# A softmax in a transformer layer divides its probabilities before they are turned, and its transposed inverse goes away

## The reference, cut to what matters

```python
def forgetting_attention(q, k, v, log_f):
    cum = jnp.cumsum(log_f, axis=-1)
    ...
        logits = jnp.einsum('bhqd,bhkd->bhqk', q_i, k).astype(jnp.float32) * scale
        logits = logits + c_i[..., :, None] - cum[..., None, :]
        logits = jnp.where(pos_i[:, None] >= kpos[None, :], logits, -jnp.inf)
        p = jax.nn.softmax(logits, axis=-1)
        return jnp.einsum('bhqk,bhkd->bhqd', p.astype(v.dtype), v)
```

## Time and profile before

| | |
|---|---|
| Time, median of 3 executions | 1922.04 us (1921.72 to 1925.91) |
| Profiled execution | 1924.92 us, its span 1923.2 us |
| Busy over the span | PE 98%, DVE 62%, POOL 44%, ACT 39% |
| Span of the attention's four pairs | about 780 to 970 us |
| Granted clock of PE over the span | 0.996 of full speed |

### The profile page before, as it was taken

The page is one execution under the profiler, slowest core; times in us unless marked ns, Lnnn a source line. Parts: engine busy times, 40 slices in busy tenths (PEclk is TensorE's granted clock), DMA queues, the critical chain, the costliest instruction groups (busy, mean ns, idle before and its releaser), DMA issues. The chain is left out here.

```text
span 1923.2 us, 25334 instructions
## 1 busy us (share of the span) xinstructions
PE 1881.0 (98%) x9240; PEld 1545.9 (80%) x9240; DVE 1184.5 (62%) x1720; ACT 758.4 (39%) x1389; POOL 842.9 (44%) x629
## 2 busy tenths in 40 slices
PE   7999999999999999999999999999999999999998
PEld 6878888888888877777788887877888888888886
DVE  6876666665777792455515567577453445358778
ACT  5632232222444442555513554244333233334445
POOL 1587777774000011222211242489887788700003
PEclk9999999999999999999999999999999999999999
DMA  9246656654976310311112112622422333168662
GB/s 346 76 142 188 202 176 203 187 169 135 350 261 193 122 40 22 133 45 45 67 33 72 55 43 93 216 98 89 132 103 90 103 117 109 39 262 324 207 193 92
DMA packets 211946, 267.93 MB, mean 139 GB/s; under 512 B 14558, under 2 KB 125426, under 8 KB 211314
## 3 DMA queue, kind: packets, MB, share of 16 engines
q1 hardware_dynamic: 211826, 266.34, 41.4%
HBM read 211.16 MB, written 53.03 MB: 137 GB/s over the span
## 5 line engine op out<-in xcount | busy, mean ns | idle before, releaser
L470 POOL TENSOR_TENSOR ffn_ring_b<-ffn_raw_in,ffn_ring_b 128x512 fp32r<-128x512 f32 x146 | 207.3, 1427 | 113.0 <-ACT ffn_ring_b L465 113.0
L1127 PE MATMUL bank<-ffn_w_hi,ffn_a_hi 128*128 128x512 f32 x616 | 240.2, 390 | 1.3 <-DVE ffn_w_lo L1093 1.2
L1129 PE MATMUL bank<-ffn_w_hi,ffn_a_lo 128*128 128x512 f32 x616 | 239.7, 389 | 0.0
L1128 PE MATMUL bank<-ffn_w_lo,ffn_a_hi 128*128 128x512 f32 x616 | 239.7, 389 | 0.0
L111 POOL TENSOR_SCALAR rms<-rms 128x1 f32<-128x1 f32 x20 | 9.4, 470 | 435.6 <-ACT ffn_junk L103 421.6
L465 ACT CAST ffn_ring_b<-ffn_raw_in 128x512 fp32r<-128x512 f32 x150 | 92.5, 621 | 217.6 <-PE bank L1652 210.8
L1082 ACT CAST ffn_a_hi<-ffn_a_stage 128x512 fp32r<-128x512 f32 x154 | 95.6, 621 | 199.0 <-PE bank L1129 194.2
L470 POOL TENSOR_TENSOR ffn_ring_a_lo<-ffn_raw_in,ffn_ring_a_hi 128x512 fp32r<-128x512 f32 x106 | 146.1, 1390 | 55.5 <-ACT ffn_ring_a_hi L465 53.4
L1441 DVE TENSOR_TENSOR ffn_u<-bank,ffn_u 128x512 f32<-128x512 f32 x106 | 72.9, 688 | 126.4 <-PE bank L1652 126.1
L1093 DVE TENSOR_TENSOR ffn_a_lo<-ffn_a_stage,ffn_a_hi 128x512 fp32r<-128x512 f32 x154 | 106.2, 690 | 68.5 <-ACT ffn_a_hi L1082 68.3
L1127 PEld LDWEIGHTS bank<-ffn_w_hi,ffn_a_hi 128*128 128x128 f32 x616 | 115.6, 188 | 26.9 <-DVE ffn_w_lo L1093 2.0
(11 more groups left out here) (416 smaller groups left out, 4725.3 us busy)
## 6 DMA issues: line engine op xcount, KB each, us to landing
ffn_raw_in<-in_w_ffn_in SPq DMA_DIRECT2D x84, 512.0 KB, 5.8
ffn_a_stage<-hidden SPq DMA_DIRECT2D x154, 256.0 KB, 3.2
ffn_w_stage<-in_w_ffn_out SPq DMA_DIRECT2D x132, 256.0 KB, 3.1
ada_rest<-in_w_ada SPq DMA_DIRECT2D x64, 448.0 KB, 4.0
hidden<-ffn_u SPq DMA_DIRECT2D x87, 256.0 KB, 2.0
hidden<-ffn_g SPq DMA_DIRECT2D x66, 256.0 KB, 2.0
mx_raw_w<-in_w_mix_in SPq DMA_DIRECT2D x28, 512.0 KB, 4.4
xres<-in_x SPq DMA_DIRECT2D x16, 512.0 KB, 8.5
```

What stands on the lines that cost most here:

```text
L470: pool.tensor_tensor(self.lo(q), self.source(b, m), self.hi(q).bitcast(F32), ALU.subtract)\
L1127: pe.matmul(dst, a_hi, w_hi, start=first, stop=False, skip_group_check=True)
L1128: pe.matmul(dst, a_hi, w_lo, start=False, stop=False, skip_group_check=True)
L1129: return pe.matmul(dst, a_lo, w_hi, start=False, stop=True, skip_group_check=True)
```

## The change

Each tile of probabilities is divided by its row sums on DVE, in place, between the exponential and the turning: `scale_prob(p, n)` waits for `exp_rows`, takes the inverse of one column of `rowsum`, waits for it, and multiplies the tile. `turn_prob` waits for this (`prob_scaled`) and no longer for the exponential. `invert`, `turn_rinv` and `keep_rinv` are gone, with the semaphores of theirs, and `normalise` becomes `keep_y_fox`, a copy. On PE, steps 2 to 5 are written like steps 6 and 7: values first, then both turnings.

```diff
-            def keep_rinv(p, q, first):
-                act.wait_ge(pv_ready, p * NS + (q + 1))
...
-                act.copy(rinv[:, 2 + q % 2, :], core.bank[:, 6 + q % 2, P:2 * P]).then_inc(rinv_kept, 1)
...
-            def invert(p, q, first):
...
-                dve.reciprocal(rinv[:, q % 2, :].rearrange("p (e d) -> p e d", e=2),
-                               rowsum[:, 2 * q:2 * q + 2].unsqueeze(2).to_broadcast([P, 2, HD]))\
-                    .then_inc(rinv_made, 1)
+            def scale_prob(p, n):
+
+                dve.wait_ge(prob_done, p * PER + (n + 1))
+                rows = prob[:, n % RP, 0:(BLOCK[n] + 1) * P]
+                link(dve.reciprocal(rinv[:, n:n + 1], rowsum[:, n:n + 1]))
+                dve.tensor_scalar(rows, rows, rinv[:, n:n + 1], None, ALU.mult).then_inc(prob_scaled, 1)
...
+            def keep_y_fox(p, q):
                 i = BLOCK[2 * q]
...
+                dve.tensor_copy(yT_fox[:, bass.ds(p, 1), i * P:(i + 1) * P].rearrange("p a s -> p (a s)"),
+                                core.bank[:, 6 + q % 2, 0:P]).then_inc(y_done, 1)
 
             def fox_body(p, first, last):
                 link.at(p)
                 for q in range(1, NS + 1):
                     if not last and q < NS and q - 1 in STEP_OF:
                         cut_qk(p + 1, STEP_OF[q - 1])
+                    scale_prob(p, 2 * q - 2)
                     if q < NS:
                         logits(p, 2 * q, first)
+                    scale_prob(p, 2 * q - 1)
                     keep_pt(p, 2 * q - 2, first)
                     if q < NS:
                         logits(p, 2 * q + 1, first)
-                    invert(p, q - 1, first)
                     keep_pt(p, 2 * q - 1, first)
...
             def turn_prob(p, n, first):
                 i = BLOCK[n]
-                pe.wait_ge(prob_done, p * PER + (n + 1))
+                pe.wait_ge(prob_scaled, p * PER + (n + 1))
...
-            def turn_rinv(p, q):
-                bank = core.bank[:, 6 + q % 2, :]
-                pe.wait_ge(rinv_made, p * NS + (q + 1))
-                pe.transpose(bank[:, P:2 * P], rinv[:, q % 2, :], core.ident[:, :]).then_inc(pv_ready, 1)
...
                     scores(p, q, first)
-                    if q in (6, 7):
+                    if q == 1:
+                        turn_prob(p, 0, first)
+                        project_q0(p, first, range(KD - 2, KD))
+                    else:
                         values(p, q - 2, first)
-                        turn_rinv(p, q - 2)
                         turn_prob(p, 2 * q - 2, first)
-                    else:
-                        turn_prob(p, 2 * q - 2, first)
-                        if q == 1:
-                            project_q0(p, first, range(KD - 2, KD))
-                        else:
-                            values(p, q - 2, first)
-                            turn_rinv(p, q - 2)
                     turn_prob(p, 2 * q - 1, first)
```

More of the change, by code:

```diff
@@ L1872, in mixer @@
     pv_ready, y_done = s("pv_ready"), s("y_done")
-    rinv_made, rinv_kept = s("rinv_made"), s("rinv_kept")
+    prob_scaled = s("prob_scaled")
     x_ready, x_kept = s("x_ready"), s("x_kept")
@@ L1917, in mixer @@
     rowsum = fsb("rowsum", [P, 2 * NS])
-    rinv = core.at("mx_rinv", [P, 4, P], 120)
+    rinv = fsb("rinv", [P, 2 * NS])
     wait_tile = fsb("wait_tile", [P, 2 * NS])
@@ L2227, in keep_pt @@
                 act.copy(pt_of(n, 0, w), turned_bank(n, 0)[:, 0:w]).then_inc(pt_act, 1)
-            def keep_rinv(p, q, first):
-                act.wait_ge(pv_ready, p * NS + (q + 1))
-                if not (first and q < 2):
-                    act.wait_ge(y_done, p * NS + (q - 1))
-                act.copy(rinv[:, 2 + q % 2, :], core.bank[:, 6 + q % 2, P:2 * P]).then_inc(rinv_kept, 1)
             def fox_body(p, first, last):
@@ L2423, in keep_pt @@
                 dve.tensor_copy(pt_of(n, BANK, w), core.bank[:, 5, 0:w - BANK]).then_inc(pt_dve, 1)
-            def invert(p, q, first):
-                dve.wait_ge(prob_done, p * PER + (2 * q + 2))
-                if not (first and q < 2):
-                    dve.wait_ge(pv_ready, p * NS + (q - 1))
-                dve.reciprocal(rinv[:, q % 2, :].rearrange("p (e d) -> p e d", e=2),
-                               rowsum[:, 2 * q:2 * q + 2].unsqueeze(2).to_broadcast([P, 2, HD]))\
-                    .then_inc(rinv_made, 1)
-            def normalise(p, q):
-                dve.wait_ge(rinv_kept, p * NS + (q + 1))
+            def scale_prob(p, n):
[4 more added lines that the diff above has]
+            def keep_y_fox(p, q):
                 i = BLOCK[2 * q]
-                dve.tensor_tensor(yT_fox[:, bass.ds(p, 1), i * P:(i + 1) * P].rearrange("p a s -> p (a s)"),
-                                  core.bank[:, 6 + q % 2, 0:P], rinv[:, 2 + q % 2, :], ALU.mult).then_inc(y_done, 1)
+                dve.wait_ge(pv_ready, p * NS + (q + 1))
+                dve.tensor_copy(yT_fox[:, bass.ds(p, 1), i * P:(i + 1) * P].rearrange("p a s -> p (a s)"),
+                                core.bank[:, 6 + q % 2, 0:P]).then_inc(y_done, 1)
             def fox_body(p, first, last):
@@ L2456, in fox_body @@
                     if q > 1:
-                        normalise(p, q - 2)
-                normalise(p, NS - 1)
+                        keep_y_fox(p, q - 2)
+                keep_y_fox(p, NS - 1)
                 if not last:
@@ L2703, in values @@
                     for e in range(2):
-                        pe.matmul(bank[e * HD:(e + 1) * HD, 0:P], v_fox[:, j, bass.ds(p * (2 * HD) + e * HD, HD)],
-                                  pt_of(2 * q + e, j * P, (j + 1) * P), start=(j == 0), stop=(j == i))
-            def turn_rinv(p, q):
-                bank = core.bank[:, 6 + q % 2, :]
-                pe.wait_ge(rinv_made, p * NS + (q + 1))
-                pe.transpose(bank[:, P:2 * P], rinv[:, q % 2, :], core.ident[:, :]).then_inc(pv_ready, 1)
+                        mm = pe.matmul(bank[e * HD:(e + 1) * HD, 0:P],
+                                       v_fox[:, j, bass.ds(p * (2 * HD) + e * HD, HD)],
+                                       pt_of(2 * q + e, j * P, (j + 1) * P), start=(j == 0), stop=(j == i))
+                mm.then_inc(pv_ready, 1)
             def first_mv(t, ks):
@@ L2749, in fox_body @@
                 values(p, NS - 1, first)
-                turn_rinv(p, NS - 2)
-                turn_rinv(p, NS - 1)
                 if not last:
```

3 lines of the change are left out of this document (removed).

## The result

The changed kernel takes 1949.95 us (median; 1947.71 to 1953.81), beside 1923.97 us (1921.72 to 1926.17) for the kernel before in the same session: a ratio of 1.0136, 95% interval [1.0122, 1.0149], so 26.0 us more. A second session gave 1949.57 against 1925.03 us, 1.0129 [1.0113, 1.0144]. Forecast were +18.3 us and at most 1948: the direction was right, the size too small, and the range missed. The profiled execution took 1953.81 us, its span 1952.1.

A forecast was written before the change was run, and what follows sets the result against it. PE was taken to bound the kernel, busy 49.95 of 50.30 us in the second pair. Terms -4.4 - 2.1 + 10.8 + 2.6 + 5.6 + 5.8 = +18.3 us on 1922.0 gave 1940.3 us, range 1931 to 1948.

The forecast's parts named there:

- turned inverses gone: On PE, each step's transposed inverse of 0.17 us goes; with the pair-start exceptions, -4.4 us together.
- second turnings behind ACT, one change of kind less: Steps 2 to 4: second turning waits 0.90 us for ACT's copy, +10.8; steps 2 to 5: fewer changes of work, -2.1.
- scaling in steps 1, 6, 7, without POOL (1.6 + 5.8): PE waits for DVE's scalings: 1.6 us in step 1 over four pairs, 5.8 in steps 6 and 7 of three pairs.
- exclusion by POOL, steps 1 and 2 (1.0 + 5.6): DVE's scaling waits until POOL's L1962 ends: 1.0 us in step 1, 5.6 us in step 2 over four pairs.
- clock: PE's granted clock: no cost in the sum; a fall to 0.79 appeared only as 4 us in rival 2.
- rival 2: More on top: register waits 3.2 us, clock falls behind products using few array rows 4; +25.5, 1947.5 us; chance 0.12, shared.
- rival 4: DVE scales at full rate, 1.224 us at 1024 columns: some 1.5 us more per pair, 1946 us; shares rival 2's 0.12.
- rival 1: No exclusion of DVE's scaling by POOL: sum without 5.6 and 1.0, +11.7, 1933.7 us; chance 0.27.
- the two waits of the last pair: Two PE waits of a few tenths of a us in the last pair, left out of the sum.
- where this cover holds: Steps 3 to 5: scalings run on DVE while PE does scores and values, so they cost nothing.
- not slower (3): PE does not wait at second turnings of steps 2 to 4: +1.9, 1924 us, or faster, 1915.5; chance 0.09.
- register waits in the looped pairs: Two looped pairs: each wait first takes its value from a register, 0.1 us per scaling, 1.6 per pair, 3.2 in all.

The follow-up runs named there:

- POOL short: Changed kernel with POOL's L1962 in the attention's steps 1 and 2 cut to 8 of 1024 columns: 1941.66 us, 1.0089 of the kernel before.
- the last experiment but one: Changed kernel with DVE's cut of the next pair's projection moved behind the second scaling in steps 6 and 7: 1945.82 us, 1.0105 of the kernel before.
- the kernel with four pieces: Changed kernel with POOL's low part of the weights in steps 1 and 2 formed in four 256-column instructions: 1942.50 us, 1.0087 of the kernel before.

## Why the prediction was wrong

| step of the sum | forecast | in the traces' attention |
|---|---|---|
| turned inverses gone | -4.4 | -2.39 |
| second turnings behind ACT, one change of kind less | +8.7 | +9.40 |
| scaling in steps 1, 6, 7, without POOL (1.6 + 5.8) | +7.4 | +8.02 |
| exclusion by POOL, steps 1 and 2 (1.0 + 5.6) | +6.6 | +5.33 |
| clock | 0 | +6.20 |
| sum | +18.3 | +26.56 |

The right column is the difference of the attention's length from each kernel to the next in the order of the table; its last difference is split by the waits.

**The step that failed is that the sum keeps the granted clock at 1.00.** The forecast worked out a wait of over 2 us in step 2 of each pair and then priced it at its length. The fall stood in rival 2 only, at 1 us per pair and with a chance of 0.12 that it shared with rival 4, and was put down to "products that used few rows of the array". The runs show that PE's wait can bring it, with POOL's long instruction or without; that in the attention it came behind 14 of 18 waits of 1.78 to 2.15 us in five profiled executions, and behind none of the many of up to 1.13 us (between 1.13 and 1.78 nothing was tried); and that one costs 1.5 us. It came behind 3 of the 4 waits of step 1, which follow a projection, and behind 11 of the 14 of step 2, which follow transposes, so it is not tied to the transposes. With 4 x 1.5 the sum would have been 24.3, near the 24.5 and 26.0 measured. The nearness is in part luck, since the number of falls in the executions behind the medians is not known (above).

The trace of the kernel before could have given this price a place in the sum. Outside the attention PE has waits of this length there too, and one of them has its fall; the last two rows are of one place, before and changed:

```profile
1198.66 0.77 PE L3068 MATMUL bank<-mx_wo_hi,h_hi 128*128 128x512 f32 x1 [1.98 <-PEq L65]
1198.60:1203.60 5.00, 4.94 (x12) 3.95 (x13) 2.94 (x2) 4.96 (x6) 3.84 (x2) 0.50 0.79 261
...
714.95 1.06 PE L146 MATMUL bank<-ident,ffn_xn_b 128*128 128x128 f32 x8 [2.58 <-DVE h_lo L164]
...
716.43 1.94 PE L146 MATMUL bank<-ident,ffn_xn_b 128*128 128x128 f32 x8 [2.58 <-DVE h_lo L164]
```

Behind 1.98 us the clock is 0.50 for 5 us. At the other place the same wait of 2.58 us, far from the change, is followed by eight transposes in 1.06 us in one execution and in 1.94 us in the other (granted clock 1.00 and 0.67). And the 0.79 of the earlier trace rows has no long wait ahead of it, only 0.31 and 0.69 us between small products (730.60 to 732.64). So the length of one wait is not all that decides; what else does is open.

**Two terms were mis-sized.** The turned inverse is worth 0.10 us and not 0.17: its start-to-start time held 0.07 of a change of kind that stays when it goes. At a pair's start the forecast was right that nothing is won: PE now waits 0.59 us for the cut of the keys there instead of 0.23. And the two waits of the last pair, "left out", are 0.69 us together; they are most of the 0.7 by which the order cost more than forecast.

**Right were** the mechanisms, by their rows. The second turning waits start to start as worked out, and at all twelve places (in step 2 of pairs 2 to 4 DVE's copy comes later still). The scaling is held up by POOL: the TENSOR_SCALAR of 896 columns takes 2.46 us (forecast some 2.5), so rival 1 falls. The trace agrees with the rule of the Trainium skill weighed there, "GPSIMD Engine Reference", Key points, that POOL contends with DVE instructions in a 2-port perf mode: 2.46 us against 0.69. The price came otherwise than worked out, 5.33 and not 6.6. In step 2 of pairs 2 to 4 the wait grew by 1.38, 1.32 and 1.32 us (forecast 1.4 each). In step 1 of these pairs the scaling took 0.75 to 0.84 us and the step grew by at most 0.09 (forecast 0.26), since the hindered scaling ends some 0.5 us behind POOL and not its full length. In the first pair the forecast had the places wrong: 1.31 us in step 1 and nothing in step 2. Steps 6 and 7, scaled with POOL short, are 0.98 and 1.12 longer than without scaling in the same order, 2.10 against 1.94, and the last experiment but one shows that the cut ahead of the scaling is why: with the scalings first they are 7.96 and 9.38, near the 7.88 and 9.13 without scaling. Steps 3 to 5 cost nothing for the scaling "where this cover holds": in the old order, without the cover, they cost 0.4 to 0.55 each.

**Of the rivals,** not slower (3) falls: PE waits at all the places. A scaling at full rate (4) falls: 0.69 us for 896 columns. Rival 2 had the fall, underpriced, and behind small products where the runs show it behind waits. Its first half, register waits in the looped pairs, shows as 0.80 us behind ACT in pairs 2 and 3 against 0.72 in pairs 1 and 4, 0.08 at two places of each looped pair, not 1.6 per pair. That its +25.5 lies so near the 26.0 is luck: 3.2 of it are these register waits.

## What to carry to other kernels

Taking work off the engine that bounds is worth nothing if the work that replaces it lies in the chain that this engine waits for: here 2.5 us came back from PE, and the order and DVE's scalings, with what POOL and the clock added, cost ten times that. Price a wait on PE by its length and by what the clock does behind it, and look for waits that several small delays on one engine make long together. Parts of a change are not additive when one covers another; undo them in both orders before blaming one.

## What was not expected of the hardware

- The same wait of about 2 us was followed by a fall of PE's clock in some places and not in others: by a clock of 0.66 in one pair and 1.00 in another of one program (1.97 and 2.06 us; also 2.15 and 2.08). One fall costs 1.5 us in the attention.
- A TENSOR_SCALAR in SBUF is held up by POOL's TENSOR_TENSOR, 2.46 us for 0.69, but DVE's copy out of PSUM is not: 0.56 us beside POOL's pieces in the kernel with four pieces, 0.56 at 844.90 beside the whole L1962 of the kernel before, and 0.55 alone.
- Four pieces of 256 columns take POOL 2.81 to 3.26 us, one of 1024 takes 2.35 to 2.39.
